# Half of the cached keys turned by VectorE instead of TensorE, and half of the attention products computed by GpSimd

## The chip, the cores and the metric

The kernel runs on one core of a Trainium2 chip. The metric is the device time of one execution in microseconds (us); lower is better. Times of a version are given as the median of several runs.

## The reference, cut to what matters

The reference is one decoder layer over two groups of tokens: a prompt of 2048 tokens, and eight sample sequences of 4 new tokens each with 4096 cached tokens. The part that the change touches is the stick-breaking attention with 8 heads of 64:

```
z = q.k / sqrt(64) + bias_h
A[t,s] = sigmoid(z_ts) * prod_{s<j<t} (1 - sigmoid(z_tj))   for s < t, else 0
o = A v
```

The product over later keys is a running product from the newest key to the oldest. For the sample group, keys and values of the past lie in a cache of pages of 128 tokens (each a block of 128 rows of 512 numbers); a page table of 8 x 32 numbers says where they are. Projections, a gated recurrence, a routed mixture of experts and norms make up the rest of the layer and are not touched, except for a few instructions of the sample group's projection.

## The kernel before, in words

The program is a row of stages: modulation, projection of the prompt, projection of the sample group (`sample_projection_phase`, from L622), attention (`attention_phase`, from L846, the trace's 703 to 1506 us), output projection and routing, experts, final norm. In each stage the five engines run their own lists of instructions and meet at semaphores. Every engine takes its list strictly in order.

**Prompt attention.** It is cut into 320 items, one per tick n: a pair of heads, a tile of 128 queries, a chunk of up to 512 keys, one of the two heads. 192 items are 512 keys wide by position away from the diagonal; the 128 on the diagonal are 128, 256, 384 or 512 wide. Each item passes these steps:
- TensorE makes the scores in a bank `zb` (L1291, for two items at once in every second tick).
- ScalarE makes two sigmoids: `leave`, 1 minus the probability (L1135), and `take`, the probability (L1137).
- VectorE scans `leave` from right to left as a running product into `left` (L1253). The scan's start value is column 512 of `left`: 1 on the diagonal (a memset, L1150), else a copy of column 0 of the item four ticks earlier (L1152, `first`).
- VectorE multiplies `take` by `left` shifted by one column (L1159, `weights`) in the next tick.
- TensorE turns the product in up to four 128x128 transposes into a bank `tb` (L1304, `turn`), two ticks after the scores' tick.
- The turned weights are copied to `wT`: by VectorE for every fourth item (L1168), by ScalarE for the others (L1067).
- TensorE multiplies them with the values into `ob` (L1326), once for two items.

There are four buffers each of `take`, `leave` and `left`, three banks `zb` and three banks `tb`. The banks `tb` go round over a list EVENTS that fixes the order of all turns, and names for each the engine that empties it.

**Sample attention** is laid between the ticks of the prompt's. A unit is 512 cached tokens of four sequences at once, and takes 19 ticks (WINDOW); p is the tick within the unit, and there are 16 units. For p from 0 to 15 TensorE turns the unit's keys, one bank of four 128x128 blocks in a tick (`k_turn`, L1339): sequence p // 4, columns 128 (p % 4) to +128 of its four pages. VectorE copies the bank to `kTs` for p = 3, 7 and 11 (L1175), ScalarE for the other 13 (L1074). In p = 17 TensorE makes the unit's scores with 32 matrix instructions in a row (L1349). ScalarE makes two sigmoids of them (L1087, L1088), VectorE a scan and a product (L1200, L1203), and in the next unit TensorE turns the weights (L1357) and multiplies them with the values in p = 4, 7, 10 and 13 (L1366).

**Transfers.** SyncE loads the key pages, four to a buffer, two buffers, one DMA of 128 rows of 2 KB each per page (`page`, L954). A buffer is loaded again when TensorE has turned its last block. Between them SyncE issues zeros for two tables in memory (`zero_rows`, L972 and L973), and at the end of units 1, 4 and 8 the next pair's queries, keys and values (`load`, L964 to L968), which wait for TensorE. GpSimd does nothing in the loop but issue the DMAs of the value pages, four at a time (L1056), when TensorE is through with the buffer.

**Sample projection.** TensorE projects the 32 new tokens into one bank (L725), VectorE copies it to `proj` (L770), TensorE turns that by 128 columns at a time into `pT` (L741), and VectorE copies from there the new keys to `kT_new` (L793) and the new queries, each head's rows in its own place among zeros, to `q_blk` (L798, eight copies).

Of the kernel before, what the change touches and what calls it, by code (L numbers as in the profile page):

```python
# [63 lines left out]
SHIFT1, SCALE1 = 0, KC  # L64
WCOL = {"q": 0, "k": WA, "v": 2 * WA, "xr": 3 * WA, "yb": 3 * WA + WR}


def ds(start, size):
    return bass.ds(start, size)
# [552 lines left out]
def sample_projection_phase(nc, io, keep, sems):  # L622
# [4 lines left out]
    with ExitStack() as stack:  # L627
# [17 lines left out]
        ps = {n: k.ps(f"ps3_{n}", [P, 512]) for n in ("pj", "pv", "pT", "g", "rms", "mod0", "mod1")}  # L645
        s = {n: k.sem(f"p3_{n}") for n in ("pj", "pv", "pje", "pT", "ext", "row", "xc",
# [8 lines left out]
        def part(name):  # L655

            return ps["pT"][:, :].rearrange("p (f j t) -> p f j t", f=FC, j=4)[:, :, PARTS.index(name), :]
# [5 lines left out]
        with nc.Block() as block:  # L663
# [33 lines left out]
            def _(act):  # L697
                act.wait_ge(s["gp"], 1)
# [23 lines left out]
            def _(pe):  # L722
# [19 lines left out]
                mm.then_inc(s["pT"], 1)  # L742
                modulation(0, 2, KC)
# [22 lines left out]
            def _(dve):  # L766
# [26 lines left out]
                dve.tensor_copy(seqs(keep["kT_new"]), part4("k"))  # L793
                for pair in range(H // 2):
                    for half in range(2):
                        rows = slice(64 * half, 64 * half + 64)
                        c0 = (2 * pair + half) * TS
                        dve.tensor_copy(keep["q_blk"][rows, :, pair, c0:c0 + TS],  # L798
                                        part("q")[rows, pair, :].rearrange("p (b t) -> p b t", b=BS))
# [46 lines left out]
def attention_phase(nc, io, keep, sems):  # L846
# [13 lines left out]
    FIRST, WINDOW, TICKS = 3, 19, N + 8  # L860

# [5 lines left out]
    for n in range(TICKS):  # L867
        unit, p = place(n)
        if 2 <= n < N + 2:
            EVENTS.append((("turn", n - 2), "dve" if (n - 2) % 4 == 0 else "act"))  # L870
# [6 lines left out]
        if p < 4 * FC and 0 <= unit < NU:  # L877
            EVENTS.append((("k_turn", unit, p), "dve" if p in (3, 7, 11) else "act"))
# [6 lines left out]
    with ExitStack() as stack:  # L885
# [8 lines left out]
        leave = [k.sb(f"leave{i}", [P, GRP]) for i in range(4)]  # L894
# [3 lines left out]
        kp = [keep["w_out"][:, 0, PPC * i:PPC * i + PPC, :] for i in range(2)]  # L898
# [24 lines left out]
        s_kp = [k.sem(f"p5_k{i}") for i in range(2)]  # L923
# [25 lines left out]
        def page(eng, which, dst, sem, u, j):  # L949

            first = (4 * (u // NY) + j) * NPAGES + (NY - 1 - u % NY) * PPC
            for i in range(PPC):
                number = eng.value_load(pages[0:1, first + i:first + i + 1], min_val=0, max_val=NPHYS - 1)
# [1358 lines left out]
```

## Time and profile before

| | |
|---|---|
| median of 3 runs | 2825.01 us (2823.09 to 2826.18) |
| the profiled execution's own time | 2821.11 us |
| its span, first to last instruction | 2819.6 us |
| mean granted TensorE clock | 0.969 of full speed |
| attention stage in it | about 703 to 1506 us |

Busy times of an engine are the time in which at least one of its instructions is running. In the tables of rows each line is a group of like instructions: source line, engine, operation, what is written from what, shape, count, then busy time and mean duration of one, and behind the next bar the idle time of the engine just before them with what ended it.

### The profile page before, as it was taken

What the parts mean: (1) busy time and instruction counts of PE and PEld (TensorE: products, weight loads), DVE (VectorE), ACT (ScalarE), POOL (GpSimd) and SP (SyncE); (2) the same over time, 40 slices, a digit from 0 to 9 for tenths busy, and PEclk for the clock granted to TensorE, in tenths of its full rate; (3) what the DMA queues carried; (4) which work ended last, traced back from release to release, by engine and by line L of the source; (5) the groups of instructions that cost most, each with busy time, mean ns of one, the idle gap of its engine ahead of it and who ended that gap; (6) DMA issues with size and microseconds to landing.
All of it is one profiled execution on the core that took longest, in us unless ns stands there. A gap on an engine that the chain in (4) does not pass through costs nothing. (4 is left out here: it accounts for less than half of the span.)

```text
span 2819.6 us, 64656 instructions
## 1 busy us (share of the span) xinstructions
PE 2586.6 (92%) x23589; PEld 1361.0 (48%) x23589; DVE 1379.9 (49%) x2816; ACT 1055.4 (37%) x1938; POOL 648.4 (23%) x918
## 2 busy tenths in 40 slices
PE   6999999996799899899998999789999998899978
PEld 3444444442455445454543555445555554555533
DVE  2151423333678788687886777522222222222228
ACT  2221314121677777687773222122222221122214
POOL 0202020101021211111111222343333333333333
PEclk9999999998899999999999999899999999999989
DMA  9011111126586766767675344399999789999947
GB/s 335 15 61 44 45 45 43 62 85 244 174 271 218 264 234 224 262 213 244 225 262 187 116 140 139 143 261 295 281 301 299 210 257 306 323 309 297 305 134 315
DMA packets 297027, 577.06 MB, mean 205 GB/s; under 512 B 80278, under 2 KB 96727, under 8 KB 292812
## 3 DMA queue, kind: packets, MB, share of 16 engines
q1 hardware_dynamic: 194472, 427.99, 47.4%
q0 software_dynamic: 102016, 146.26, 16.9%
q8 instruction: 116, 1.90, 0.3%
q14 instruction: 99, 0.81, 0.1%
q10 hardware_dynamic: 324, 0.10, 0.0%
HBM read 461.12 MB, written 112.29 MB: 203 GB/s over the span
## 5 line engine op out<-in xcount | busy, mean ns | idle before, releaser
L1253 DVE TENSOR_TENSOR_SCAN left<-leave,left 128x512 f32<-128x512 f32 (+3 forms) x320 | 358.4, 1120 | 134.9 <-ACT leave L1135 134.1
L442 PE MATMUL bank<-xnT,w_in 128*128 128x512 f32 x768 | 330.3, 592 | 0.0
L2056 DVE TENSOR_TENSOR sg<-sg,bank 128x128 f32<-128x128 f32 x160 | 46.0, 288 | 562.5 <-ACT sg L1992 561.3
L2023 PE MATMUL bank<-w,hT 128*32 128x256 f32 x5120 | 297.5, 380 | 1.5 <-issue 1.1
L1056 POOL DMA_DIRECT2D w_out<-in_cache_v x256 | 137.6, 538 | 660.9 <-issue 658.6
L1935 POOL DMA_DIRECT2D rowsP<-xs_d x328 | 218.0, 665 | 200.0 <-DMA rowsP<-xs_d 111.4
L2016 PE MATMUL bank<-w,o_sq 128*32 128x256 f32 x3840 | 218.0, 384 | 30.2 <-DVE o_sq L2051 23.2
L442 PEld LDWEIGHTS bank<-xnT,w_in 128*128 128x128 f32 x768 | 145.6, 190 | 181.8 <-issue 178.9
L1992 ACT ACTIVATE sg<-bank 128x128 f32<-128x128 f32 x160 | 44.4, 278 | 501.2 <-PE bank L2016 501.2
L1619 PE MATMUL bank<-w_out,w 128*128 128x512 f32 x512 | 227.7, 597 | 1.8 <-DVE w L1683 1.8
L442 PE MATMUL bank<-w_in,xnT 128*128 128x512 f32 x512 | 220.4, 592 | 0.0
L2023 PEld LDWEIGHTS bank<-w,hT 128*32 128x32 f32 x5120 | 160.1, 110 | 124.2 <-DVE hT L2060 25.7
L2016 PE MATMUL bank<-oT,o_sq 128*32 128x256 f32 x3712 | 205.8, 379 | 7.1 <-DVE o_sq L2051 7.1
L1304 PE MATMUL tb<-ident,take 128*128 128x128 f32 x1088 | 181.7, 284 | 29.5 <-DVE take L1159 25.7
L1135 ACT ACTIVATE leave<-zb,nbiasP 128x512 f32<-128x512 f32 (+3 forms) x320 | 204.6, 639 | 8.0 <-PE zb L1297 8.0
L1137 ACT ACTIVATE take<-zb,biasP 128x512 f32<-128x512 f32 (+3 forms) x320 | 207.3, 648 | 0.0
L1159 DVE TENSOR_TENSOR take<-take,left 128x512 f32<-128x512 f32 (+3 forms) x320 | 194.6, 608 | 15.5 <-DVE left L1253 0.4
L1949 POOL DMA_DIRECT2D ys_d<-y x164 | 115.6, 709 | 365.3 <-DMA ys_d<-y 180.8
L1291 PE MATMUL zb<-w 64*128 64x512 f32 (+3 forms) x640 | 164.1, 590 | 31.0 <-ACT take L1137 19.9
L1304 PEld LDWEIGHTS tb<-ident,take 128*128 128x128 f32 x1088 | 119.8, 142 | 146.7 <-issue 77.4
L1339 PE MATMUL tb<-ident,w_out 128*128 128x128 f32 x1024 | 159.9, 280 | 25.3 <-DMA w_out<-in_cache_k 15.7
L2016 PEld LDWEIGHTS bank<-w,o_sq 128*32 128x32 f32 x3840 | 125.2, 111 | 118.2 <-DVE o_sq L2051 26.3
(408 smaller groups left out, 3402.1 us busy)
## 6 DMA issues: line engine op xcount, KB each, us to landing
w_out<-in_cache_v POOLq DMA_DIRECT2D x256, 256.0 KB
w_out<-in_cache_k SPq DMA_DIRECT2D x256, 256.0 KB
w<-in_w SPq DMA_DIRECT2D x128, 512.0 KB, 17.4
w<-in_w SPq DMA_DIRECT2D x22, 2048.0 KB, 23.1
oT<-in_w SPq DMA_DIRECT2D x22, 2048.0 KB, 24.2
w_out<-in_w SPq DMA_DIRECT2D x20, 2048.0 KB, 25.7
ys_d<-zeros SPq DMA_DIRECT2D x32, 816.0 KB
ys_d<-y POOLq DMA_DIRECT2D x166, 128.0 KB, 7.8
```

What stands on the lines that cost most here:

```text
L442: mm = pe.matmul(ps[:, :], w, m, start=(i == 0), stop=(i == len(parts) - 1))
L1135: act.activation(leave[n % 4][:, 0:cols], zb[n % 3][:, 0:cols], ACT.Sigmoid, scale=-SCALE, bias=keep["nbiasP"][:, head:head + 1]).then_inc ...
L1137: act.activation(take[n % 4][:, 0:cols], zb[n % 3][:, 0:cols], ACT.Sigmoid, scale=SCALE, bias=keep["biasP"][:, head:head + 1]).then_inc(s_ ...
L1159: dve.tensor_tensor(take[n % 4][:, 0:cols], take[n % 4][:, 0:cols], left[n % 4][:, 1:cols + 1], ALU.mult).then_inc(s_w, 1)
L1253: dve.tensor_tensor_scan(left[n % 4][:, 0:cols][:, ::-1], leave[n % 4][:, 0:cols][:, ::-1], leave[n % 4][:, 0:cols][:, ::-1], left[n % 4][ ...
L1291: mm = pe.matmul(zb[(n + par) % 3][:, 0:cols], qT[pair % 2][half, t * P:t * P + P], kT[pair % 2][half, c * GRP:c * GRP + cols], start=True ...
L1304: mm = pe.transpose(to[:, j * P:j * P + P], take[n % 4][:, j * P:j * P + P], ident[:, :])
L1339: mm = pe.transpose(to[:, i * P:i * P + P], kp[g % 2][:, i, f * P:f * P + P], ident[:, :])
L1619: mm = pe.matmul(pb[half][0:n, :], lhs, w_out[:, half, c, :], start=(c == 0), stop=(c == KC - 1))
L1935: return pool.dma_start(x_in[64 * half:64 * half + 64, buffer, u * (XW // 2):(u + 1) * (XW // 2)].rearrange("p a n -> p (a n)"), in_strips ...
L2016: mm = pe.matmul(h[u][q * Q:q * Q + Q, 0:2 * P], xT[:, c, u, :], w13[i][:, c, :, q * P:q * P + P], start=(c == 0), stop=(c == KC - 1))
L2023: mm = pe.matmul(yb[q * Q:q * Q + Q, u * (XW // 2):(u + 1) * (XW // 2)], hT[:, u, j, :], w2[i][:, j, q * (XW // 2):(q + 1) * (XW // 2)], s ...
```

## The change

- **Keys.** The key pages go through eight slots of one page each (`kp`, SLOTS). PAGES gives the order within a unit: in even p a page of sequence 0 or 1, in odd p a page of sequence 2 or 3 (TURNED = 2). A page of sequences 2 and 3 is loaded as before and turned by TensorE in four 128x128 blocks into one bank, which ScalarE copies. A page of sequences 0 and 1 is loaded with four DMAs, each of 32 tokens, whose rows of 2 KB are cut into four pieces of 512 bytes that land on four strips of 32 partitions. VectorE then turns the page in one instruction, 128x512, which transposes each 32x32 block by itself. The score matmuls read it through a view (`keys`) with runs of 32 columns.
- **New keys and queries of sequences 0 and 1 of each four** are laid out to match the strips: ScalarE makes a second, rearranged copy of `proj`, TensorE turns it into a bank `pC`, and VectorE copies queries in 16 small copies from there, besides eight from `pT`.
- **Products.** `weights` of items with odd n moves to GpSimd; even ones stay on VectorE.
- **Scan.** `leave` has one column more, set to 1 once; off the diagonal the scan is 513 wide and takes its start value straight from column 0 of `left`, and the copy of L1152 is gone.
- **Copies.** All copies of turned weights are ScalarE's, and all key banks (eight a unit instead of sixteen) too.
- **Value pages.** GpSimd issues them in two halves, two DMAs in the tick after the buffer's last use and two in the tick after that, between its products.

```diff
-            EVENTS.append((("turn", n - 2), "dve" if (n - 2) % 4 == 0 else "act"))
+            EVENTS.append((("turn", n - 2), "act"))
...
-            EVENTS.append((("k_turn", unit, p), "dve" if p in (3, 7, 11) else "act"))
+        if p < 4 * PPC and 0 <= unit < NU and PAGES[p][0] >= TURNED:
+            EVENTS.append((("k_turn", unit, p), "act"))
...
+    PAGES = [(j + TURNED * side, i) for j in range(TURNED) for i in range(PPC) for side in range(2)]
+    SLOTS, VALUES = 8, (4, 7, 10, 13)
...  SyncE
+                        if j < TURNED:
+                            for strip in range(STRIPS):
+                                sp.dma_start(dst[:, strip * P:strip * P + P],
+                                             src[:, strip * Q:strip * Q + Q, :].rearrange("a t (s n) -> s (a t) n", n=P)).then_inc(landed, 16)
+                        else:
+                            sp.dma_start(dst, src.rearrange("a p n -> (a p) n")).then_inc(landed, 16)
...  GpSimd
+                def weights(n):
+                    cols = item(n)[4]
+                    pool.wait_ge(s_tk, n + 1)
+                    pool.wait_ge(s_sc, n + 1)
+                    pool.tensor_tensor(take[n % 4][:, 0:cols], take[n % 4][:, 0:cols], left[n % 4][:, 1:cols + 1], ALU.mult).then_inc(s_wp, 1)
...
+                for n in range(TICKS):
+                    if n % 2 == 0 and 0 <= n - 1 < N:
+                        weights(n - 1)
+                    for late, samples in ((1, (0, 1)), (2, (2, 3))):
+                        u, p = place(n - late)
+                        if p in VALUES and 1 <= u <= NU:
+                            g = PPC * (u - 1) + VALUES.index(p) + 2
+                            if g < PPC * NU:
+                                v_pages(g, samples)
...  VectorE
+                def scanned(n):
+                    _, t, c, _, cols = item(n)
+                    dve.wait_ge(s_lv, n + 1)
+                    if c == t // TPG:
+                        dve.wait_ge(s_in, sum(item(m)[2] == item(m)[1] // TPG for m in range(n + 1)))
+                        size, carry = cols, left[n % 4][:, cols:cols + 1]
+                    else:
+                        multiplied(n - 4)
+                        size, carry = GRP + 1, left[n % 4][:, 0:1]
+                    dve.tensor_tensor_scan(left[n % 4][:, 0:size][:, ::-1], leave[n % 4][:, 0:size][:, ::-1], leave[n % 4][:, 0:size][:, ::-1],
+                                           carry, ALU.mult, ALU.bypass).then_inc(s_sc, 1)
...
                 def k_turn(u, p):
...
-                    dve.tensor_copy(kTs[p // FC][:, p % FC, :], bank("k_turn", u, p)[:, :]).then_inc(s_cd, 1)
+                    dve.transpose(kTs[j].rearrange("p f n -> p (f n)")[:, i * GRP:i * GRP + GRP], rows).then_inc(s_kd, 1)
...
-                    if 0 <= n - 1 < N:
+                    if 0 <= n - 1 < N and n % 2:
                         weights(n - 1)
...  TensorE, turn
-                    pe.wait_ge(s_w, n + 1)
+                    pe.wait_ge(s_wp if n % 2 else s_w, n // 2 + 1)
```

## Rows read from the trace of the kernel before

**Rows 1.** Stretches of the run: start:end, length, busy by engine, clock, DMA share, GB/s.
```profile
703.00:1506.00 803.00, 719.16 (x5177) 390.50 (x5175) 642.26 (x1156) 597.26 (x1176) 137.41 (x256) 0.97 0.69 232
```
**Rows 2.** Groups of the attention stage, by shape.
```profile
L1253 DVE TENSOR_TENSOR_SCAN left<-leave,left 128x512 f32<-128x512 f32 x224 | 286.6, 1280 | 84.4 <-ACT leave L1135 83.9
L1159 DVE TENSOR_TENSOR take<-take,left 128x512 f32<-128x512 f32 x224 | 154.0, 688 | 8.9
L1168 DVE COPY wT<-tb 128x512 f32<-128x512 f32 x48 | 32.7, 680 | 0.0
L1152 DVE COPY left<-left 128x1 f32<-128x1 f32 x192 | 24.6, 128 | 0.0
L1339 PE MATMUL tb<-ident,w_out 128*128 128x128 f32 x1024 | 159.9, 280 | 25.3 <-DMA w_out<-in_cache_k 15.7 <-DVE wT L1168 7.0 <-ACT wT L1067 1.1
L1349 PE MATMUL tb<-rowsP,q_blk 128*32 128x512 f32 x256 | 59.6, 609 | 1.7 <-ACT wT L1067 1.7
```
**Rows 3.** Timeline of VectorE: start, duration, instruction.
```profile
1254.56 0.68 DVE L1159 TENSOR_TENSOR take<-take,left 128x512 f32<-128x512 f32 x1
1255.15 1.28 DVE L1253 TENSOR_TENSOR_SCAN left<-leave,left 128x512 f32<-128x512 f32 x1
1256.54 0.69 DVE L1159 TENSOR_TENSOR take<-take,left 128x512 f32<-128x512 f32 x1
1257.14 1.28 DVE L1253 TENSOR_TENSOR_SCAN left<-leave,left 128x512 f32<-128x512 f32 x1
...
1259.14 1.28 DVE L1253 TENSOR_TENSOR_SCAN left<-leave,left 128x512 f32<-128x512 f32 x1
...
1260.38 0.68 DVE L1168 COPY wT<-tb 128x512 f32<-128x512 f32 x1
1260.97 0.68 DVE L1159 TENSOR_TENSOR take<-take,left 128x512 f32<-128x512 f32 x1
1261.57 1.27 DVE L1253 TENSOR_TENSOR_SCAN left<-leave,left 128x512 f32<-128x512 f32 x1
```
**Rows 4.** Timeline of TensorE over the same ticks.
```profile
1255.31 1.13 PE L1291 MATMUL zb<-w 64*128 64x512 f32 x4
1256.37 0.66 PE L1304 MATMUL tb<-ident,take 128*128 128x128 f32 x4
1256.86 0.60 PE L1339 MATMUL tb<-ident,w_out 128*128 128x128 f32 x4
1257.30 0.64 PE L1304 MATMUL tb<-ident,take 128*128 128x128 f32 x4
...
1259.36 1.13 PE L1291 MATMUL zb<-w 64*128 64x512 f32 x4
```
**Rows 5.** Timeline of ScalarE over the same ticks.
```profile
1255.12 0.62 ACT L1074 ACTIVATE rowsP<-tb 128x512 f32<-128x512 f32 x1
1255.60 0.72 ACT L1135 ACTIVATE leave<-zb,nbiasP 128x512 f32<-128x512 f32 x1
1256.17 0.73 ACT L1137 ACTIVATE take<-zb,biasP 128x512 f32<-128x512 f32 x1
```
**Rows 6.** TensorE's waits for key pages: start, duration, instruction, idle before it.
```profile
956.53 1.11 PE L1339 MATMUL tb<-ident,w_out 128*128 128x128 f32 x4 [8.48 <-DMA w_out<-in_cache_k]
```
**Rows 7.** A transpose of VectorE, and a product of GpSimd, from other stages: count, min/median/max ns.
```profile
L2051 DVE STREAM_TRANSPOSE o_sq<-o_rs x162: 400/424/447, 1841.9 to 2723.2; 128x256 f32<-128x256 f32 x162
L617 POOL TENSOR_TENSOR gt<-gt,yb x4: 4509/4512/4514, 106.1 to 557.0; 128x2048 f32<-128x2048 f32 x4
```
**Rows 8.** Timeline of GpSimd, issuing value pages.
```profile
1257.77 0.54 POOL L1056 DMA_DIRECT2D w_out<-in_cache_v  x1 [0.61 <-issue]
1258.91 0.54 POOL L1056 DMA_DIRECT2D w_out<-in_cache_v  x1 [0.60 <-issue]
```
**Rows 9.** Projection stage, timeline of GpSimd and of VectorE beside it.
```profile
256.38 4.51 POOL L617 TENSOR_TENSOR gt<-gt,yb 128x2048 f32<-128x2048 f32 x1
...
256.83 0.69 DVE L573 COPY qk_st<-bank 128x512 f32<-128x512 f32 x1 [24.50 <-PE bank L442]
```
**Rows 10.** DMA queues: packets, MB, share of 16 engines; 740 to 1460 us, then 1850 to 2700 us.
```profile
q1 hardware_dynamic: 59237, 106.05, 44.0%
...
q0 software_dynamic: 67030, 41.51, 20.4%
```
**Rows 11.** Sample projection, timeline of VectorE.
```profile
673.98 1.59 DVE L798 COPY q_blk<-ps_pT 64x32 f32<-64x32 f32 x8
680.97 0.29 DVE L811 TENSOR_TENSOR ig_s<-ig_s,xc_s 128x128 f32<-128x128 f32 x1 [4.38 <-ACTq L711]
```

More of the change, by code:

```diff
@@ L742, in _ @@
                 mm.then_inc(s["pT"], 1)
+                pe.wait_ge(s["pce"], 1)
+                for f in range(FC):
+                    mm = pe.transpose(ps["pC"][:, f * P:f * P + P], proj_c[:, f * P:f * P + P], ident[:, :])
+                mm.then_inc(s["pC"], 1)
                 modulation(0, 2, KC)
@@ L797, in _ @@
                         c0 = (2 * pair + half) * TS
-                        dve.tensor_copy(keep["q_blk"][rows, :, pair, c0:c0 + TS],
-                                        part("q")[rows, pair, :].rearrange("p (b t) -> p b t", b=BS))
+                        dve.tensor_copy(keep["q_blk"][rows, :, pair, c0:c0 + TS].rearrange("p (a j) t -> p a j t", j=4)[:, :, TURNED:],
+                                        fours(part("q")[rows, pair, :], "p")[:, :, TURNED:])
                 dve.wait_ge(s["sig"], 1)
@@ L893, in attention_phase @@
         take = [k.sb(f"take{i}", [P, GRP]) for i in range(4)]
-        leave = [k.sb(f"leave{i}", [P, GRP]) for i in range(4)]
+        leave = [k.sb(f"leave{i}", [P, GRP + 1]) for i in range(4)]
         left = [k.sb(f"left{i}", [P, GRP + 1]) for i in range(4)]
@@ L897, in attention_phase @@
         pages = k.sb("pages", [1, BS * NPAGES], I32)
-        kp = [keep["w_out"][:, 0, PPC * i:PPC * i + PPC, :] for i in range(2)]
+        kp = [keep["w_out"][:, 0, i, :] for i in range(SLOTS)]
         vp = [keep["w_out"][:, 1, PPC * i:PPC * i + PPC, :] for i in range(2)]
@@ L947, in bank, with page, k_page, keys @@
             return tb[EVENT[name] % 3]
[L949 to L953, printed above, removed]
-                eng.dma_start(dst[:, i, :], cache[which][ds(number, 1)].rearrange("a p n -> (a p) n")).then_inc(sem, 16)
+        def page(eng, u, j, i):
+            at = (4 * (u // NY) + j) * NPAGES + (NY - 1 - u % NY) * PPC + i
+            return eng.value_load(pages[0:1, at:at + 1], min_val=0, max_val=NPHYS - 1)
+        def k_page(u, p):
+            g = 4 * PPC * u + p
+            return kp[g % SLOTS], s_kp[g % SLOTS], (g // SLOTS + 1) * (16 * STRIPS if PAGES[p][0] < TURNED else 16)
+        def keys(j, f):
+            if j < TURNED:
+                return kTs[j].rearrange("p f n -> p (f n)").rearrange("p (b f r) -> p f b r", f=FC, r=Q)[:, f]
+            return kTs[j][:, f, :]
         with nc.Block() as block:
@@ L1046, in _, with v_pages @@
                 pool.drain().then_inc(s_band, 1)
-                pool.wait_ge(s_pg, 16)
-                for g in range(PPC * NU):
+                def v_pages(g, samples):
                     u, i = divmod(g, PPC)
@@ L1227, in _ @@
                 dve.memset(left_n[:, TS:], 1.0)
+                for i in range(4):
+                    dve.memset(leave[i][:, GRP:], 1.0)
+                dve.drain()
                 first(0)
                 for n in range(TICKS + 1):
-                    if 0 <= n - 3 < N and (n - 3) % 4 == 0:
-                        turn(n - 3)
                     u, p = place(n - 1)
@@ L1249, in _ @@
                     if n < N:
[L1250 to L1254 removed]
+                        scanned(n)
                     if n == 1:
```

118 lines of the change are left out of this document (65 added, 53 removed).

## The prediction, made before the changed kernel ran

> **What bounds the kernel now.** The page's sums say TensorE is busy for 92% of the span, but the change touches one stage, so the first view is the busy time by stretch. From 703 to 1506 us TensorE is busy 719.2 of 803 us, VectorE 642.3, ScalarE 597.3, GpSimd 137.4 and the DMA engines 69% [rows 1]. Two engines lie near the length of the stage, so the groups are read next, and then a stretch of the timeline, for "busy" leaves out the small gaps between instructions.
>
> In the timeline VectorE runs back to back. A tick with only scan and product takes 1257.14 to 1259.14, that is 2.00 us; a tick with one more 512-column copy takes 1259.14 to 1261.57, 2.43 us [rows 3]. A unit of 19 ticks has about 4.75 copies of turned weights and 3 of keys on VectorE, so 19 x 2.00 + 7.75 x 0.43 = 41.3 us at full width, and the unit's own scan and product (about 2 us). TensorE is as full: two ticks, from scores to scores, take 1255.31 to 1259.36, 4.05 us, or 2.03 a tick [rows 4], and the units' value matmuls and the scores of L1349 come on top; the latter are a block of some 3.7 us in each unit (59.6 us over 16) [rows 2]. Per unit 719.2 / 16 = 45.0 us of a stage that gives each 50.2 (803 / 16). In the block's shadow VectorE runs dry, since no new `leave` comes: part of its 83.9 us of waits [rows 2]. So neither engine alone sets the pace: VectorE does between the blocks, TensorE in them. A change that relieves only one would be paid badly. This one relieves both.
>
> **TensorE.** Removed are 512 of the 1024 transposes of L1339. Together they are busy 159.9 us [rows 2], so half is 80 us, which agrees with 0.47 us per bank in the timeline (8 banks x 16 units x 0.47 = 60; with the loads and hand-offs about it up to 80) [rows 4]. I take 80 as the ceiling and 60 as the floor. Matmul shapes are otherwise the same; that the moving keys are read in runs of 32 columns is shown by no row. Bounds: 0, and for the 256 instructions on those keys half again of 59.6 us, 30 us [rows 2]. I take 0, since the same number of columns streams. TensorE's own need becomes about 719 - 80 = 639 us.
>
> **VectorE.** Removed: 80 copies of turned weights and 48 of keys at an interval of 0.60 us at full width (1260.38 to 1260.97) [rows 3], 128 x 0.60 = 77 less about 10 for narrow ones, so 67 us; 160 products, half of L1159's, 154.0 / 2 = 77 at full width, with the narrow ones about 97 by duration and 85 by interval [rows 2, 3]; 192 start copies, 24.6 us by duration, which overlap the scan's tail, and 0.1 us each in effect, 19 us [rows 2, 3]. Together about 171. Added: 128 transposes of 128x512. The trace has 128x256 at 424 ns [rows 7]; a full-width product has 688 [rows 2], and I take 0.69 by duration and 0.60 by interval, since a copy and a product of one size cost alike here. Bounds 0.60 and 0.85 (twice 424). So 128 x 0.60 = 77. The scan's one column more costs nothing to speak of. Net about -94 us; a pair of ticks goes from 4.4 to 2 x 1.20 (scans) + 0.60 + 0.60 + about 0.1 = 3.7, 1.85 a tick.
>
> **ScalarE.** It gets 80 copies of weights and loses 80 of keys (208 to 128): nothing. Its pace is 2 x 0.57 for the sigmoids and 0.48 for a copy [rows 5]: 1.14 + 0.48 + 0.24 = 1.86 a tick.
>
> **GpSimd.** 160 products are added. 2048 columns take 4.51 us [rows 7], so 512 take 1.13, and with a fixed part about 1.17: 187 us less the narrow ones, 165. It stands idle now but for DMA issues at 1.14 us apart [rows 8]; together 165 + 256 x 1.14 = 457 us of 803. In the middle of a unit it is tight: three ticks bring four issues (4.6 us) and 1.5 products (1.8), 6.4 us, or 2.13 a tick. A product behind four issues starts up to 4.6 us late; behind it stands TensorE, which turns in order, and behind that the sigmoids four items on. The list gives it one tick more than the scan needs, and TensorE needs there about 2.03 - 0.24 + 0.33 = 2.12 a tick itself. So I count no loss between them but jitter.
>
> What VectorE and GpSimd do to each other when both read their operands at once is shown by no row: GpSimd's products in the projection ran beside single-operand copies of VectorE, none of them stretched [rows 9]. Bounds: nothing, and one whole product of waiting on VectorE for each on GpSimd, 160 x 1.17 = 187 us. I take nothing, the end nearest to the even 4.51 us [rows 7]; the other is the first rival.
>
> The Trainium skill, "SBUF — State Buffer", section "Who interferes with whom", says that a VectorE instruction with two SBUF inputs contends with a GpSimd instruction that reads SBUF, and that the second to issue fully blocks. Scan and product both have two such inputs, so by that rule the sum is the first rival's.
>
> **Transfers.** Half of the key pages, 128, now make 512 packets of 512 bytes instead of 128 of 2 KB: 65,536 for 16,384. In this stage a packet of 1.79 KB costs 0.440 x 720 x 16 / 59,237 = 86 ns; in the expert stage one of 0.62 KB costs 0.204 x 850 x 16 / 67,030 = 41 ns [rows 10]. At 41 ns that is 168 us on 16 engines for 98 before, at 86 ns 352. I take 41, the nearer size: DMA share 0.69 + 70 / 803 = 0.78. Eight slots of one page give each a lead of 8 ticks, about 17 us, where a buffer of four pages was reloaded in one go. The long waits for pages are behind the loads of the next pair, the longest 8.48 us [rows 6]; the loads keep their place, so the waits stay, now partly on VectorE. Where a page is late, scans are queued behind VectorE's wait and everything behind them; before, only TensorE's own list was.
>
> The Trainium skill, "DMA: Bandwidth & Descriptors", "Specifications", gives 512 bytes as the least size at line rate. By that alone the pieces would cost no more per byte than rows of 2 KB, and the sum would be the same with a share of 0.69; the rate of the small packets above (15 GB/s per engine against 21) speaks against it.
>
> **Sample projection.** Sixteen more small copies at 0.2 us (1.59 / 8) and one of keys make +3.4 us on VectorE, where 4.38 us of waiting follow [rows 11]: hidden. TensorE's extra turn after ScalarE's copy delays the gates by about 1 us: +1. Without that cover it would be +4.
>
> **The sum.** TensorE keeps 639 us of work and idles 84 us now, of which some 20 are the stage's start and 17 the late pages. If all waits stay, the stage shortens by 80; jitter with GpSimd's queue and three engines at 1.85 to 2.1 a tick will give some of it back, and I take three quarters, 60. Then 2821.1 - 60 + 1 = 2762 on the profiled execution; the median shown lies 3.9 above that execution, so 2766. The case's own range is 2742 (all of the 80) to 2790 (35).
>
> **Rivals.**
> - *VectorE and GpSimd take turns at the operands.* Place: every odd item's product. Price: in two ticks the shared reads are two scans (2.56), a product (0.69) and GpSimd's 1.17, 4.4 us with no gaps: 2.2 a tick, what VectorE needs today (2.00 to 2.43). And GpSimd, waiting about 0.65 (half a scan) before each product, needs 1.5 x 1.8 + 4.6 = 7.3 us in three ticks, 2.44 a tick over 11 of 19: +2.7 us a unit at worst. That is 0 to +44 us, +15 as its middle, for TensorE's relief is worth nothing then: about 2840. It decides from 60 / 160 = 0.37 us of blocking per product. For it: every scan and product has two operands in SBUF. Against: no row shows it.
> - *Part of that:* blocking of 0.2 us or so per product, or late products that hold TensorE. About -20: 2806.
> - *Small packets.* At 86 ns per packet the engines would need 0.69 x 803 + 254 = 808 us of 803: pages late on VectorE, and the stage 10 us longer: 2836. For it: peaks of the DMA share are at 1 already after a load. Against: the 41 ns row, and a queue that is idle between bursts.
> - *The change does not relieve what paces it:* an item's way through five engines and three banks sets 2.2 a tick whatever each costs. Against: in the timeline VectorE and TensorE are back to back, and idle is not spread. Within 5 us of now.
>
> **How the numbers follow.** Forecast 0.52, blocking in full 0.22, in part 0.12, packets 0.07, no relief 0.07. A change of 0.2% (5.6 us) is what can be told from none here. Faster: 0.52, nearly all of the part case (0.10), and 0.01 of others, 0.63. Same: 0.11, from no relief and the near end of blocking. Slower: 0.26. The range leaves 0.1 out at each end: 2738, just below the full 80 us, to 2848, most of the way through the blocking case.
>
> **What would show it.** Right: the attention stage about 745 us; TensorE busy near 640 in it; VectorE's tick near 1.9 us between blocks; transposes near 0.69 and GpSimd's products at 1.1 to 1.2 us, with VectorE's scans still at 1.28 and no gaps before them. Wrong: products of GpSimd stretched over 1.5 us, or scans stretched to 2 us and more; waits of TensorE's turns for GpSimd; VectorE's transposes waiting for pages; DMA share near 0.9; score matmuls on strips above 0.6 us.

## The result, and the profile after

The changed kernel takes 3080.43 us (median of 3 runs, 3073.80 to 3084.99) against 2825.01 us before: a ratio of 1.090, 95% interval 1.087 to 1.094. The forecast was 2766 with a range to 2848; the time lies 232 us above the range.

The stretches first, with the columns of [rows 1]: the attention stage ends near 1765 us instead of 1506, and inside it TensorE, VectorE, ScalarE and the DMA engines are each busy for a smaller share than before.
```profile
703.00:1765.00 1062.00, 731.39 (x4651) 362.01 (x4653) 611.20 (x802) 592.91 (x1175) 304.13 (x415) 0.85 0.57 176
```
TensorE is busy 731 of 1062 us at a granted clock of 0.85, VectorE 611, and the DMA share fell from 0.69 to 0.57. None of them is full in the mean, so something else is late. The groups of the stage by shape say what (they answer to [rows 2]):
```profile
L1229 DVE TENSOR_TENSOR_SCAN left<-leave,left 128x513 f32<-128x513 f32 x192 | 267.3, 1395 | 120.9 <-ACT leave L1198 120.4
...
L1105 POOL TENSOR_TENSOR take<-take,left 128x512 f32<-128x512 f32 x112 | 132.8, 1187 | 352.6 <-DVE left L1229 336.0 <-ACT take L1200 15.9
L1237 DVE TENSOR_TENSOR take<-take,left 128x512 f32<-128x512 f32 x112 | 86.7, 775 | 6.6
...
L1404 PE MATMUL tb<-ident,w_out 128*128 128x128 f32 x512 | 91.4, 308 | 242.0 <-DMA w_out<-in_cache_k 241.8 <-ACT wT L1129 0.2
L1245 DVE STREAM_TRANSPOSE rowsP<-w_out 128x512 f32<-128x512 f32 x128 | 89.4, 699 | 221.7 <-DMA w_out<-in_cache_k 221.7
...
L1414 PE MATMUL tb<-rowsP,q_blk 128*32 128x512 f32 x256 | 62.7, 635 | 0.0
```
TensorE waits 241.8 us for key pages (before: 15.7, [rows 2]) and VectorE 221.7 us, largely at the same times. Two smaller things stand there too: the scans take 1395 ns instead of 1280 and VectorE's products 775 instead of 688.

The pages are issued by SyncE, which the prediction had not read. Its instructions, count: min/median/max ns; L1036 is the four DMAs of a page on strips, L1039 the plain one, L974 the load of a page number:
```profile
L1036 SPq DMA_DIRECT2D w_out<-in_cache_k x512: 537/585/13382, 713.3 to 1716.3; - x171
L974 SPq TENSOR_LOAD <-pages x256: 268/760/1648, 711.9 to 1716.9; - x128
L1039 SPq DMA_DIRECT2D w_out<-in_cache_k x128: 331/336/1339, 717.5 to 1718.5; - x128
```
and its timeline (start, duration, instruction):
```profile
1098.13 3.47 SPq L1036 DMA_DIRECT2D w_out<-in_cache_k  x4
1102.90 0.34 SPq L1039 DMA_DIRECT2D w_out<-in_cache_k  x1
1104.00 2.84 SPq L1036 DMA_DIRECT2D w_out<-in_cache_k  x4
1108.13 0.33 SPq L1039 DMA_DIRECT2D w_out<-in_cache_k  x1
1109.26 3.24 SPq L1036 DMA_DIRECT2D w_out<-in_cache_k  x4
```
A pair of pages takes 5.3 to 5.9 us here (1098.13 to 1104.00 to 1109.26), and two ticks, which use up a pair, last 4.0 to 4.9 us [rows 3]. Over the whole stage it is 8.3 us a pair (1062 us for 128 pairs). SyncE waits for a freed slot only 22 us in the whole stage. The view of the queues over 1098 to 1114 us shows the result (DMA: tenths of busy time in 40 slices; GB/s in the same slices):
```profile
DMA  9884322222222268952221222224986022221122
GB/s 174 282 283 106 99 85 74 83 85 86 79 78 78 77 105 198 293 181 68 81 82 56 82 82 81 67 72 105 138 298 225 28 67 82 70 81 53 49 84 76
```
Whenever little but strips' pages is under way, 75 to 85 GB/s arrive and the 16 DMA engines are two tenths busy in the mean. That can be all of them short of work, or a few of them full; which it is, the experiments and a count of packets below decide.

### The profile page after: what moved, and what is told of

The parts are those of the page before. It is cut to its first block and busy times, and to the rows that moved or that the text cites. A ratio compares the mean times of both kernels' runs of the same rounds, so it can differ in the third digit from the quotient of the medians.

```text
span 3083.5 us, 64688 instructions
## 1 busy us (share of the span) xinstructions
PE 2602.1 (84%) x23081; PEld 1335.3 (43%) x23081; DVE 1353.7 (44%) x2485; ACT 1052.4 (34%) x1939; POOL 817.9 (27%) x1078
## 5 line engine op out<-in xcount | busy, mean ns | idle before, releaser
L1229 DVE TENSOR_TENSOR_SCAN left<-leave,left 128x513 f32<-128x513 f32 (+4 forms) x320 | 392.5, 1228 | 213.0 <-ACT leave L1198 211.2
L1404 PE MATMUL tb<-ident,w_out 128*128 128x128 f32 x512 | 91.4, 308 | 242.0 <-DMA w_out<-in_cache_k 241.8
L1105 POOL TENSOR_TENSOR take<-take,left 128x512 f32<-128x512 f32 (+3 forms) x160 | 165.1, 1033 | 489.2 <-DVE left L1229 472.3
L1129 ACT ACTIVATE wT<-tb 128x512 f32<-128x512 f32 (+3 forms) x320 | 173.3, 542 | 178.7 <-PE tb L1371 178.0
L1371 PEld LDWEIGHTS tb<-ident,take 128*128 128x128 f32 x1088 | 127.0, 150 | 186.1 <-issue 77.6
L1358 PE MATMUL zb<-w 64*128 64x512 f32 (+3 forms) x640 | 177.6, 635 | 35.1 <-ACT take L1200 23.9
```

The source lines that it names most:

```text
L1105: pool.tensor_tensor(take[n % 4][:, 0:cols], take[n % 4][:, 0:cols], left[n % 4][:, 1:cols + 1], ALU.mult).then_inc(s_wp, 1)
L1129: act.activation(wT[m % 2][par][:, 0:cols // P, t % 2, :], bank("turn", n)[:, 0:cols].rearrange("p (j q) -> p j q", q=P), ACT.Copy).then_i ...
L1229: dve.tensor_tensor_scan(left[n % 4][:, 0:size][:, ::-1], leave[n % 4][:, 0:size][:, ::-1], leave[n % 4][:, 0:size][:, ::-1], carry, ALU.m ...
L1358: mm = pe.matmul(zb[(n + par) % 3][:, 0:cols], qT[pair % 2][half, t * P:t * P + P], kT[pair % 2][half, c * GRP:c * GRP + cols], start=True ...
L1371: mm = pe.transpose(to[:, j * P:j * P + P], take[n % 4][:, j * P:j * P + P], ident[:, :])
```

## The experiments

In each table row below the time is a median, the ratio is against the kernel before in the same job, with its 95% interval; "products on VectorE" means that `weights` of odd items is back on VectorE.

### Which half of the change: `keys_only`, `products_only`, `rest_only`

```diff
 keys_only, rest_only:  weights(n) on VectorE for every n
 products_only, rest_only:
-TURNED = 2
+TURNED = 0
```


> The change with all products back on VectorE; the strips and their DMAs stay. Theory I (issue): SyncE's list of DMA issues paces the attention stage, 5.25 us for each pair of pages plus the zeros; then the time stays at 3080, between 3050 and 3100, and waits for key pages still sum to over 400 us. Theory S (sharing): VectorE and GpSimd block each other at the operands; then the time falls by 100 us or more, below 2980. Theory P (packets): the 512-byte pieces are slow on the DMA engines; stays at 3080 as well.

> The change with no keys on VectorE (TURNED = 0, all pages loaded by one DMA of 2 KB rows and turned by TensorE), products half on GpSimd, the copies all on ScalarE. Theories I and P: the 255 us are gone, and VectorE's relief is left, 2790 to 2820. Theory S: most of the loss stays, over 2900.

> The change with neither keys nor products moved: eight one-page slots, scans of 513 columns without the start copy, and all copies of banks on ScalarE. VectorE loses 67 + 19 = 86 us, ScalarE gains 27, TensorE the same. If VectorE paces the ticks between the blocks, 2785 to 2810; if TensorE does, 2815 to 2830. Against the kernel with the products half on GpSimd (2856.7) it gives the price of these products: 30 us or more by theory S.

| kernel | us | ratio |
|---|---|---|
| keys_only (strips, products on VectorE) | 3074.54 | 1.087 (1.085 to 1.089) |
| products_only (all keys on TensorE, products half GpSimd's) | 2856.72 | 1.011 (1.010 to 1.013) |
| rest_only (slots, 513-wide scans, all copies on ScalarE) | 2828.50 | 1.001 (0.999 to 1.003) |

Nearly all of the loss comes with the keys. GpSimd's products cost 28 us by themselves (2856.7 - 2828.5); no theory of products_only had its time in range. And rest_only, in which VectorE is busy 583 instead of 642 us and TensorE as before, gains nothing. But it is not free of a new wait: TensorE's matmuls with the samples' values wait 33 us for value pages, where they waited 1.6 before. First the kernel before, then rest_only:
```profile
L1366 PE MATMUL s_ob<-w_out,s_wT 128*32 128x512 f32 x512 | 68.2, 605 | 1.6 <-DMA w_out<-in_cache_v 1.6
```
```profile
L1426 PE MATMUL s_ob<-w_out,s_wT 128*32 128x512 f32 x512 | 71.5, 631 | 33.3 <-DMA w_out<-in_cache_v 33.3
```

### Packets, or DMAs: `one_issue_512`, `one_issue_2k`, `keys_free`

One DMA for each of VectorE's pages, the layout by strips left out; `keys_free` is the second of them with products on VectorE.
```diff
-for strip in range(STRIPS):
-    sp.dma_start(dst[:, strip * P:strip * P + P], src[:, strip * Q:strip * Q + Q, :].rearrange("a t (s n) -> s (a t) n", n=P))
+sp.dma_start(dst.rearrange("p (g n) -> p g n", n=P), src.rearrange("a (g t) (s n) -> (a t s) g n", t=Q, n=P))   # one_issue_512
+sp.dma_start(dst, src.rearrange("a p n -> (a p) n"))                                                             # one_issue_2k
```


> The change, but each page for VectorE comes with one DMA of 512 packets of 512 bytes instead of four DMAs of 128; it leaves out the layout by strips (the pieces land on other partitions), so the scores of those sequences are of wrongly placed keys. Bytes and packets are the same, issues fall from 640 to 256. Theory I: SyncE needs about 3.0 us a pair, the stage is paced by TensorE again, 2770 to 2830. Theory P: still over 3000, since the packets are the same.

> As the kernel with one DMA per page, but with 128 packets of 2 KB; it leaves out the layout by strips too. Both theories I and P: 2760 to 2800. The difference to the kernel with one DMA of 512 packets is the price of packet size alone: under 20 us by theory I, most of the 255 us by theory P.

> The change without both costs found so far: one DMA of 2 KB rows per page for VectorE (it leaves out the layout by strips), and all products on VectorE. If issue and sharing are the only two things that the prediction missed, what is left is what was forecast for the keys alone: VectorE loses 171 - 85 = 86 and gains 77 us, TensorE loses 80, so 2770 to 2800. If the forecast was also wrong that TensorE's relief shortens the stage, it is 2815 to 2835.

| kernel | us | ratio |
|---|---|---|
| one_issue_512 | 2850.10 | 1.007 (1.006 to 1.009) |
| one_issue_2k | 2849.07 | 1.008 (1.006 to 1.009) |
| keys_free | 2816.57 | 0.997 (0.995 to 0.999) |

512 packets of 512 bytes or 128 of 2 KB: 1 us apart, within the noise, though both are above their forecasts (2770 to 2830 and 2760 to 2800). keys_free, without GpSimd's products, is 32.5 us faster and in its second range (2815 to 2835). The rows of SyncE's queue from 740 to 1440 us (packets, MB, share of 16 engines), one_issue_512 first, keys_free second:
```profile
q1 hardware_dynamic: 100075, 100.47, 45.3%
```
```profile
q1 hardware_dynamic: 57683, 103.11, 44.7%
```
42,400 more packets, and per byte 4% more of the engines (45.3% for 100.47 MB, 44.7% for 103.11 MB). The rival "small packets" falls, and so does the 41 ns per packet that the prediction had taken from the expert stage: in the trace a packet of 512 bytes takes 27 ns at the median, one of 2 KB 84. The section "Specifications" of "DMA: Bandwidth & Descriptors" in the Trainium skill puts line rate at 512 bytes and above; these two rows agree within these 4%.

### The number of DMAs, or who issues them: `one_seq_dve`, `split_two`, `split_one`, `four_issue_2k`

My theory then was that SyncE pays per DMA. `one_seq_dve` puts one sequence of four on strips (TURNED = 1); the split kernels let idle GpSimd issue TensorE's plain key pages; `four_issue_2k` is keys_free with four plain DMAs for a page. Products are on VectorE in all four.
```diff
+sp.dma_start(dst[strip * Q:strip * Q + Q, :], src[:, strip * Q:strip * Q + Q, :].rearrange("a t n -> (a t) n"))   # four_issue_2k, 4 times
```


> One sequence of four turned by VectorE (p = 0, 4, 8, 12), three by TensorE; strips as in the change; all products on VectorE. SyncE's list per unit: 4 pages of strips at about 4.2 us and 12 plain ones at about 1.1, with 4.6 us of zeros: 34 us, below the 50 of a unit. By theory I the waits for pages go back to tens of us, and the time is 2780 to 2830. If it is above 2860, issue is not the whole reason.

> The change with strips kept and all products on VectorE, and TensorE's plain key pages issued by GpSimd, which has nothing else to do in the loop but value pages, where SyncE now issues only the strips' DMAs. Theory, SyncE's issue time: it is relieved of the plain issue, two page-number loads and their waits, about 1.2 of 5.25 us for a pair of pages; the pair then costs 4 to 4.2 us, below two ticks (4.5 us), but the loads of the next pair of heads and the zeros still stand in its queue. Expected 2830 to 2960, against 3074.5 for keys_only. Rival, the DMA engines or the landing of strip pages limits, not who issues: 3050 to 3080, no change.

> As split_two, but only one sequence of four has its keys on strips and turned by VectorE, three by TensorE from pages issued by GpSimd; products on VectorE. SyncE needs 4 x (4 issues and a page number), about 4 x 3.9 = 16 us a unit of some 45, so its issue time is out of the way. Theory: one_seq_dve (same work, all issued by SyncE, 2890.1) loses its 65 us to SyncE's issuing; here 2810 to 2835, TensorE relieved of a quarter of the key transposes. Rival, something other than issuing (late landing of strips, VectorE's place in the order): 2870 to 2900.

> keys_free (2816.6 us; one DMA of 2 KB rows for each of VectorE's pages, products on VectorE) with one edit: each of those pages comes by four DMAs, each of 32 rows of 2 KB onto 32 partitions. The layout by strips is left out, so half of the scores are of other numbers. The packets are 32 per DMA where the change has 128 of 512 bytes, and their shape is plain. Theory A, SyncE pays for each DMA that it issues, whatever its shape: four issues of 0.33 to 0.6 us and the slower page-number load behind them take SyncE's time per pair of pages near to the change's 5.25 us; time 3000 to 3080, waits of VectorE and TensorE for key pages near 200 us each. Theory B, it is the strided shape of the strips (0.54 to 0.72 us an issue where a plain one has 0.33): four plain issues are 4 x 0.33 + 0.33 + 1.2, about 2.9 us a pair, within the 4.5 us of two ticks; time 2815 to 2880, waits under 70 us each.

| kernel | us | ratio |
|---|---|---|
| one_seq_dve | 2890.08 | 1.022 (1.019 to 1.025) |
| split_two | 3019.26 | 1.068 (1.066 to 1.070) |
| split_one | 2882.03 | 1.020 (1.018 to 1.021) |
| four_issue_2k | 2819.71 | 0.998 (0.997 to 0.999) |

The theory is refuted by its own tests. Four plain DMAs per page cost 3 us (2819.7 against 2816.6). one_seq_dve needed 34 us of SyncE's time per unit by its count, of the 50 that a unit had, and yet lies above the 2860 that it had named as the mark for "issue is not the whole reason". Both split kernels miss their forecasts. In split_two SyncE has nothing but strips' DMAs and zeros to issue, and the strips' take longer each, 16 of them 26.7 us, where the shortest take 0.55:
```profile
1089.85 26.66 SPq L1036 DMA_DIRECT2D w_out<-in_cache_k  x16
```
So most of a long issue is not its own time; something behind SyncE holds it up. In split_one key pages come in time (VectorE waits 3.9 us for them), but TensorE waits 76 us for value pages, which GpSimd, taking its list in order, issues among the key pages. How much of that is their place in the list is not shown; the count of packets below applies to this run too.

### The order within the strips' DMAs: `four_wide`, `by_part`, `by_part_pool`, `one_by_part`

`four_wide` keeps the number, size and places of the packets but not their rearranged source; `by_part` brings the same bytes to the same places as the change, cut another way: a DMA holds one quarter of the columns, for 32 partitions, row by row.
```diff
-for strip in range(STRIPS):
-    sp.dma_start(dst[:, strip * P:strip * P + P], src[:, strip * Q:strip * Q + Q, :].rearrange("a t (s n) -> s (a t) n", n=P))
+    sp.dma_start(dst[:, strip * P:strip * P + P], src[:, :, strip * P:strip * P + P].rearrange("a t n -> (a t) n"))   # four_wide
+for part in range(STRIPS):                                                                                            # by_part
+    sp.dma_start(dst[part * Q:part * Q + Q, :].rearrange("t (strip n) -> t strip n", n=P),
+                 src[:, :, part * P:part * P + P].rearrange("a (strip t) n -> t (a strip) n", t=Q))
```


> keys_only (3074.5 us; strips, all products on VectorE) with one edit: each of the four DMAs of VectorE's pages takes the same 128 packets of 512 bytes onto the same 128 partitions and 128 columns, but in plain order, row r of the page to partition r, instead of piece by piece of 32 rows. The layout by strips is left out, so half of the scores are of other numbers. Theory A, it is the rearranged source (four pieces of each of 32 rows, piece by piece) that makes an issue slow: issues near 0.35 us, 2815 to 2850. Theory B, it is 128 packets in each of four DMAs, in whatever order: issues stay at 0.54 us and more, 3040 to 3085.

> keys_only with the same bytes at the same places, by four other DMAs: one for each piece (a quarter of the columns), onto 32 partitions, 128 packets of 512 bytes each, row by row and in a row strip by strip. Nothing of the computation is left out. Theory A (the order of the strips' DMAs is the cost, above all that their packets go round the 128 partitions four times): 2812 to 2850. Theory B (128 short packets per DMA cost the same in any order): 3040 to 3085. If it is near 2817, that is keys_free with the right layout, a little faster than the kernel before.

> The changed kernel, whole, with the strips' pages loaded as in by_part: half of the products on GpSimd as the change has them. Whatever by_part gives, this should lie 20 to 35 us above it, since GpSimd's products cost 28 to 33 us in the two pairs run so far (2816.6 to 2849.1, 2828.5 to 2856.7): by theory A 2840 to 2880, by theory B 3060 to 3090. Rival: beside strips the products cost nothing, as from keys_only to the changed kernel (3074.5 to 3080.4): within 8 us of by_part.

> As by_part, but one sequence of four on strips and turned by VectorE, three by TensorE; products on VectorE. By theory A the pages come in time (one_seq_dve, 2890.1, had them by the slow DMAs) and TensorE loses a quarter of the key transposes, VectorE has 64 transposes: 2812 to 2830. By theory B 2880 to 2900.

| kernel | us | ratio |
|---|---|---|
| four_wide (products on VectorE) | 2827.31 | 1.002 (1.000 to 1.003) |
| by_part (products on VectorE) | 2823.93 | 0.999 (0.998 to 1.000) |
| by_part_pool (the whole change) | 2855.79 | 1.011 (1.009 to 1.012) |
| one_by_part (one sequence of four) | 2826.44 | 1.000 (0.998 to 1.002) |

The rearranged source is the cost: keys_only to four_wide changes the source alone, keys_only to by_part source and destination in one statement, each with the same 128 packets of 512 bytes in each of four DMAs, and they are 247.2 and 250.6 us faster. The whole change with that statement (by_part_pool) is 224.6 us faster than the changed kernel. SyncE in by_part, then its timeline, then the queues from 1095 to 1111 us:
```profile
L1036 SPq DMA_DIRECT2D w_out<-in_cache_k x512: 316/317/17162, 713.2 to 1459.2; - x171
L974 SPq TENSOR_LOAD <-pages x256: 262/268/1701, 711.8 to 1459.6; - x128
```
```profile
1100.07 1.81 SPq L1036 DMA_DIRECT2D w_out<-in_cache_k  x4
1102.65 0.35 SPq L1039 DMA_DIRECT2D w_out<-in_cache_k  x1
1103.77 1.81 SPq L1036 DMA_DIRECT2D w_out<-in_cache_k  x4
```
```profile
DMA  6995598999999999998999999999999999999998
```
317 ns an issue for 585, 268 ns for a page number behind it for 760, a pair of pages in 3.70 us for 5.26, below two ticks; and the DMA engines are full where they were at two tenths.

**Where the time goes.** The traces have the start, length and size of every DMA packet, so the packets under way can be counted. In the changed kernel's stretch of strips alone it is mostly 4 or 5, each followed at once by the next; the share says the same, 0.26 of 16 engines is 4.2 (columns of [rows 1]; behind it by_part, where packets that overlap bring the share above 1):
```profile
1106.00:1109.00 3.00, 2.38 (x14) 1.04 (x15) 2.92 (x6) 3.00 (x6) 0.87 (x1) 1.00 0.26 75
```
```profile
1095.00:1111.00 16.00, 14.40 (x108) 6.87 (x106) 11.73 (x15) 11.88 (x22) 2.68 (x5) 1.00 1.04 252
```
Four engines are at work and twelve stand idle. The plain page issued at 1102.90 shows that they are the same four: 96 of its 128 packets start within 1.1 us (1103.86 to 1104.94), 8 for each of twelve engines, and the last 32 take until 1106.51, mixed with strips' packets. Over the attention stage, the share of time with just 4 or 5 packets under way, and the outermost size of the source of VectorE's page DMAs:

| kernel | outermost size | 4 or 5 under way |
|---|---|---|
| changed kernel, keys_only, split_two | 4 (the strips) | 28% |
| one_seq_dve | 4, half as many | 17% |
| split_one | 4, half as many | 10% |
| by_part, four_issue_2k | 32 | 3%, 4% |
| four_wide, one_issue_512 | 128 | 4%, 3% |
| keys_free; before | 128; none | 3% |

So a DMA whose source begins with a dimension of 4 has its packets on four engines, one of 32 or 128 on all 16. This is read from the count; the traces do not name the engines. What it costs, as an estimate from these rows: the strips' 65,536 packets take 29 ns in the mean, 120 us an engine on 16 and 480 us on each of four. With the stage's share of 0.57 of 1062 us (605 us an engine in the mean) that makes about 965 us (605 - 120 + 480) for the four and 485 for the others: the four are busy for nine tenths of the stage, the others for less than half.

SyncE's own time for the pattern is the lesser part. At the stage's start, where no issue is held up, a pair takes 5.3 us as well:
```profile
718.64 2.86 SPq L1036 DMA_DIRECT2D w_out<-in_cache_k  x4
722.78 0.34 SPq L1039 DMA_DIRECT2D w_out<-in_cache_k  x1
723.90 2.86 SPq L1036 DMA_DIRECT2D w_out<-in_cache_k  x4
```
Eight pairs and the zeros (4.6 us) are 47 us a unit, within the 50 of before; the measured unit has 66 (1062 / 16). What is over is issues that were held up: 95 of the 512 take more than 1 us, 244 us together. No run has the long issue without the four engines, so how much of the loss the issue adds by itself is not measured.

### What GpSimd's products cost: `rest_shadow`, `shadow_memset`

In both, products stay on VectorE and GpSimd does work that nobody waits for, beside 120 of the scans.
```diff
+pool.tensor_tensor(oT[:, 3, 3 * GRP:3 * GRP + cols], zeros[:, 0:cols], zeros[:, 0:cols], ALU.mult)   # rest_shadow
+pool.memset(oT[...cols], 0.0); pool.memset(oT[...cols], 0.0)                                         # shadow_memset
```


> As the kernel with neither moved, and GpSimd besides multiplies zeros by zeros into a part of oT that is written later, at the times of the odd items' products up to item 239 (120 products). No engine waits for these results but ScalarE once, near the end. Theory S (sharing): scans rise from 1.28 to about 1.4 us in the mean and the time rises by 10 to 40 us. Theory L (lateness: the products on GpSimd cost time only since they come late behind the page issues): scans stay at 1.28 us, and the time stays within 6 us of the kernel with neither.

> rest_shadow with GpSimd's 120 shadow products, which nobody waits for, replaced by two memsets each of the same columns, which read nothing from SBUF. Products stay on VectorE, all keys on TensorE as in rest_only (2828.5 us; rest_shadow 2851.7). Theory, sharing of operand reads between VectorE and GpSimd: with no reads by GpSimd the scans (513 wide) go back from 1481 to about 1285 ns, the products from 725 to 690, and the time to within 6 us of rest_only, 2823 to 2834. Rival, any busy GpSimd (its queue of value pages delayed, writes in the same memory) costs the same: 2845 to 2858, scans still above 1400.

| kernel | us | ratio |
|---|---|---|
| rest_shadow | 2851.74 | 1.009 (1.006 to 1.012) |
| shadow_memset | 2833.51 | 1.003 (1.001 to 1.004) |

The scans of rest_shadow, then of shadow_memset:
```profile
L1231 DVE TENSOR_TENSOR_SCAN left<-leave,left 128x513 f32<-128x513 f32 x192 | 284.4, 1481 | 74.2 <-ACT leave L1200 72.5
```
```profile
L1232 DVE TENSOR_TENSOR_SCAN left<-leave,left 128x513 f32<-128x513 f32 x192 | 246.4, 1283 | 102.0 <-ACT leave L1201 99.4
```
So it is GpSimd's reading of SBUF, not its being busy or late, that lengthens VectorE's scans. How, one pair of rows in by_part_pool shows, VectorE's timeline and GpSimd's:
```profile
1288.39 2.45 DVE L1229 TENSOR_TENSOR_SCAN left<-leave,left 128x513 f32<-128x513 f32 x1 [0.68 <-ACT leave L1198]
...
1291.95 1.27 DVE L1229 TENSOR_TENSOR_SCAN left<-leave,left 128x513 f32<-128x513 f32 x1
```
```profile
1288.65 1.10 POOL L1105 TENSOR_TENSOR take<-take,left 128x512 f32<-128x512 f32 x1
```
The scan that has a product beside it takes 2.45 us, its own 1.28 and the product's 1.10 and a little: they run one after the other. It is not always the scan that waits: of the 50 products in by_part_pool that start within a scan, 18 lengthen the scan (2.17 us in the mean), 20 are themselves lengthened (1.72 us for 1.10), and 12 do neither by much. The rule of "SBUF — State Buffer", section "Who interferes with whom", in the Trainium skill, was weighed in the prediction and overruled; the row agrees with it that the two contend. That the second to issue is the one that waits holds for 20 of the 50, and not for this row.

### Where TensorE's relief went: `light_by_part`, `light_before`

```diff
+end = 64 if pair >= 2 else None; tiles = 1 if pair >= 2 else NT
-sp.dma_start(qT[i][:, start:], ...)      # kT, vv alike
+sp.dma_start(qT[i][:, start:end], ...)
```


> by_part (2823.9 us) with two of the three loads of a next pair of heads made small: 64 of 2048 columns of queries and keys, one of 16 tiles of values; 5.8 MB less to move, the same number of DMAs and waits, and the second half of the prompt's attention computes on old numbers. Theory A, late pages take TensorE's relief: the waits behind the two loads (8.3, 6.4, 2.4, 5.0 and 6.6 us on TensorE) go and the time with them, 2795 to 2805, 10 us or more below light_before. Theory B, the order of the work between VectorE and TensorE sets the pace and the waits are taken from slack: 2815 to 2824, within 6 us of light_before.

> The kernel before (2825 us) with the same two loads made small. Its trace has one wait of 8.5 us for a key page behind such a load and 1.4 us for a page of values: 2815 to 2822 by both theories; it is what light_by_part is to be compared with.

light_by_part takes 2818.11 us (0.997, 0.996 to 0.999), light_before 2834.16 us (1.004, 1.003 to 1.006); both miss their ranges (2795 to 2805 and 2815 to 2822). Other numbers reach the experts in both, so their absolute times say little, and they are to be compared with each other: 16.0 us apart, where by_part and its kernel before are 1.6 apart. In the attention stage, which computes before the experts, the end of the last prompt scan shows it without that disturbance: 1503.2 us before, 1495.6 in light_before, 1510.7 in by_part, 1487.4 in light_by_part. What follows it takes 1316 us before and in by_part, 1336 and 1334 in the two light kernels. TensorE's and VectorE's waits behind one of these loads, in by_part:
```profile
964.29 1.12 PE L1402 MATMUL tb<-ident,w_out 128*128 128x128 f32 x4 [8.27 <-DMA w_out<-in_cache_k]
988.52 1.11 PE L1402 MATMUL tb<-ident,w_out 128*128 128x128 f32 x4 [6.42 <-DMA w_out<-in_cache_k]
```
```profile
963.30 0.71 DVE L1243 STREAM_TRANSPOSE rowsP<-w_out 128x512 f32<-128x512 f32 x1 [5.94 <-DMA w_out<-in_cache_k]
```
Theory A: late pages behind the next pair's loads do take part of the relief, about 14 us of time for two of the three loads (16.0 - 1.6). TensorE's wait for key pages falls from 54 to 25 us with them; before it was 15.7.

## Why the prediction was wrong, point by point

1. **The step that failed: "Transfers".** It divided the strips' packets by 16 engines ("168 us on 16 engines", share 0.78, the waits "stay"), without a row that had a DMA of this pattern. Measured: they go to four. By the estimate above they ask 480 us of each of these; with the 554 us of before (0.69 x 803), less 86 for the plain packets that they replace, the four engines need about 950 us in a stage of 803, and it took 1062. With the same number and size of packets, cut so that all 16 engines share them, the whole change is 224.6 us faster (changed kernel to by_part_pool). Size of the packets, which the prediction did price, is worth 1 us. SyncE's pace was priced at nothing too: an issue takes 0.55 us for 0.33, enough to show in a pair of pages (5.3 us for two ticks of 4.0 to 4.9), not enough for the stage. The rival on packets had the right resource, the DMA engines, but not the four, and ended at 2836.
2. **"I take nothing" for the sharing of operands.** Rival 1 was right: it gave 0 to +44 us, +15 as its middle, and with the pages on all engines the change lies at +30 (2855.8 against 2825.5). Keeping products on VectorE is 31.9 us faster (by_part against by_part_pool), 0.20 us for each of 160 products. VectorE's scans and products grow by about 66 us in by_part_pool: 192 x 0.133 for the 513-wide scans, 32 x (0.086 + 0.316 + 0.013 + 0.233) for the others, 112 x 0.123 for the full-width products, 16 x 0.37 for the sample scans. VectorE's busy time in the stage so falls by 19 us only (638.7 to 619.3), where half of by_part's 191 us of products, 95, had left it. The prediction chose the end of its bounds by a 4.51 us instruction beside single-operand copies, a row that did not have the situation in it.
3. **TensorE's relief of 60 to 80 us, three quarters of it kept.** The work did go: in by_part the key transposes are busy 83.3 us for 159.9 [rows 2]. The engine's busy time in the stage fell by 41 only (719 to 678 us), beside a granted clock of 0.94 for 0.97 and longer groups, such as 415 ns for 399 of the prompt's value matmuls. Of the time next to nothing arrived: -1.6 us with the right layout, -8.1 in keys_free. About 14 us are late pages behind two loads; the third load was left as it was. Two causes for the rest are argued, not shown. One is that with the products on VectorE its own tick is as long as before (eight ticks of keys_free from 1003.95 to 1021.42, 2.18 us each; before, the prediction's 41.3 us in 19 ticks are 2.17). The other is that TensorE waits longer for pages in every kernel with the new slots and the halved issues of value pages: 60 us for both kinds in by_part (54.2 and 6.1) and 38 in keys_free, for 17 before (15.7 and 1.6), which takes up about as much as its busy time fell. rest_only, which relieves VectorE alone and gains nothing, has 33 us of this wait as well, so it does not prove the first. No run puts the old transfers beside the moved work. That both engines relieved together would pay, which the prediction held, was not tried free of the sharing, and stays open.
4. **The single costs were right.** Transposes 0.69 forecast, 0.699 measured; GpSimd's full-width product 1.17 and 1.187; score matmuls on strips 0.595 us in by_part, as those on contiguous keys in the same run, against 0.609 [rows 2], so runs of 32 columns cost nothing, as taken; ScalarE no bound.
5. **The signs to look for.** The list of what would show it wrong had VectorE's transposes waiting for pages and scans stretched to 2 us; both came, the second in single scans (the mean is 1.40). It expected late pages with a DMA share near 0.9; the share was 0.57.

With the whole computation in it, no version here beats the kernel before by more than the measurement can tell: by_part is at 0.999 (0.998 to 1.000).

## What to carry to other kernels

How a DMA's pattern is cut decides over how many DMA engines its packets are spread, and a few full engines bound a stage while the mean share looks idle. When a load is replaced by rearranged ones, price the packets per engine and not over all 16, keep the outermost size large (32 and 128 were spread here, 4 was not), and if the pattern is new, measure one. Late data with a DMA share that stands at about a quarter points there. Long issues at the issuing engine need not be its own cost: compare the shortest with the mean (0.54 and 0.96 us here). And an operand-sharing rule is overruled only by a row that has both engines' two-operand instructions in it.

## What the runs showed of the hardware that was not expected

- A DMA of 128 packets of 512 bytes whose source begins with a dimension of 4 runs on four of the 16 DMA engines (mostly 4 or 5 packets under way, share 0.26, about 80 GB/s); the same packets with 32 or 128 outermost fill all of them (share 1.04 in by_part).
- Such a DMA takes 537 ns at least to issue, where the same packets in row order take 316, and the register load between them 760 ns at the median for 268. The longest issue took 13 us.
- One DMA of 512 packets takes about as long to issue as one of 128 (382 and 333 ns median), and a page in packets of 512 bytes instead of 2 KB cost 1 us of the kernel's time.
- A two-operand product of 128x512 on GpSimd and a scan on VectorE take turns: of 50 products that started within a scan, 18 lengthened the scan, as the one at 1288.65 by its whole 1.1 us (2.45 us), and 20 were lengthened themselves. Two memsets of the same columns add nothing to the scans (1283 ns), and 5 us to the kernel (2833.5 against 2828.5), which the noise nearly covers.
